# Four gate/up pairs in the direct form instead of six, new order lists, and three of four block differences moved to VectorE

## The reference

```
x = x + 0.5 * swiglu(rms(x, g_ffn1), w_up1, w_down1)      # FFN 1
...  projections, window attention, Fourier branch, gates, w_out ...
x = x + 0.5 * swiglu(rms(x, g_ffn2), w_up2, w_down2)      # FFN 2
out = rms(x, g_final)

swiglu(h, w_up, w_down): gate, up = split(h @ w_up, 2); (silu(gate) * up) @ w_down
```

## Time and profile before

| | |
|---|---|
| time, median of 3 runs | 988.93 us (988.77 to 989.03) |
| the profiled execution | 989.37 us, of which 987.6 us are the span of the trace |
| PE busy | 979.5 us, 99% of the span |
| VectorE, ScalarE, GpSimd busy | 681.4, 444.6, 183.1 us |
| granted TensorE clock, mean | 0.998 of full speed |

### The profile page before, as it was taken

The page is one execution under the profiler, slowest core; times in us unless marked ns, Lnnn a source line. Parts: engine busy times, 40 slices in busy tenths (PEclk is TensorE's granted clock), DMA queues, the critical chain, the costliest instruction groups (busy, mean ns, idle before and its releaser), DMA issues.

```text
span 987.6 us, 16144 instructions
## 1 busy us (share of the span) xinstructions
PE 979.5 (99%) x5788; PEld 872.9 (88%) x5788; DVE 681.4 (69%) x937; ACT 444.6 (45%) x677; POOL 183.1 (19%) x106
## 2 busy tenths in 40 slices
PE   9999999999999999999999999999999999999997
PEld 8889999999888888888888888888999999988887
DVE  5897989999544346678884564479798989943322
ACT  6534444447323235458773343443354444642322
POOL 1332434330011010000000002242333434000101
PEclk9999999999999999999999999999999999999999
DMA  7513424223433364122123343331333332343222
GB/s 220 166 43 91 123 85 127 86 85 91 133 89 94 110 167 121 55 86 64 44 76 96 106 127 100 93 106 50 101 107 103 109 90 80 106 118 100 83 62 86
DMA packets 188743, 98.26 MB, mean 100 GB/s; under 512 B 13384, under 2 KB 186520, under 8 KB 188704
## 3 DMA queue, kind: packets, MB, share of 16 engines
q1 hardware_dynamic: 186736, 94.40, 32.7%
q10 hardware_dynamic: 1968, 3.35, 0.9%
HBM read 95.61 MB, written 2.11 MB: 99 GB/s over the span
## 4 chain that ended last, share of the span: by engine, by line
PE 98%; issue 1%; DMA 0%; DVE 0%; POOLq 0%; POOL 0%; DVEq 0%
PE bank L1580 19%; PE bank L1581 19%; PE bank L1590 19%; PE bank L1684 11%; PE bank L1680 11%; PE bank L1678 11%; PE bank L1899 1%; PE bank L1800 1%; PE bank L1801 1%; PE bank L1805 1%; PE bank L1585 1%; PE bank L1887 0%; PE bank L1886 0%; PE bank L1917 0%; PE bank L1914 0%
## 5 line engine op out<-in xcount | busy, mean ns | idle before, releaser
L614 ACT ACTIVATE w_hi<-raw 128x1024 fp32r<-128x1024 f32 (+2 forms) x202 | 181.5, 902 | 232.9 <-PE bank L1590 151.6
L1040 DVE TENSOR_TENSOR w_lo<-raw,w_hi 128x1024 fp32r<-128x1024 f32 (+2 forms) x138 | 147.8, 1074 | 137.7 <-ACT w_hi L614 136.0
L1680 PE MATMUL bank<-t_lo,w_hi 128*128 128x256 f32 x896 | 224.7, 283 | 0.0
L1678 PE MATMUL bank<-t_hi,w_hi 128*128 128x256 f32 x896 | 224.6, 283 | 0.0
L1680 PEld LDWEIGHTS bank<-t_lo,w_hi 128*128 128x128 f32 x896 | 172.0, 192 | 0.2
L1678 PEld LDWEIGHTS bank<-t_hi,w_hi 128*128 128x128 f32 x896 | 172.0, 192 | 0.2
L1684 PE MATMUL bank<-t_hi,w_lo 128*128 128x256 f32 x896 | 144.0, 283 | 0.0
L1580 PE MATMUL bank<-a_hi,w_hi 128*128 128x512 f32 (+1 forms) x374 | 140.1, 379 | 0.0
L1581 PE MATMUL bank<-a_lo,w_hi 128*128 128x512 f32 (+1 forms) x374 | 139.4, 377 | 0.0
L1684 PEld LDWEIGHTS bank<-t_hi,w_lo 128*128 128x128 f32 x896 | 123.6, 192 | 0.0
L1529 POOL TENSOR_TENSOR ssum<-ssum,sq 128x512 f32<-128x512 f32 x20 | 30.6, 1528 | 498.9 <-ACT sq L651 498.9
(11 more groups left out here) (244 smaller groups left out, 1481.1 us busy)
## 6 DMA issues: line engine op xcount, KB each, us to landing
raw<-in_w_down_dram SPq DMA_DIRECT2D x48, 384.0 KB, 3.0
raw_b<-in_w_up_dram SPq DMA_DIRECT2D x64, 256.0 KB, 3.6
raw<-in_w_up_dram SPq DMA_DIRECT2D x64, 256.0 KB, 3.6
raw<-in_w_up_dram SPq DMA_DIRECT2D x24, 512.0 KB, 3.8
raw<-in_w_in_dram SPq DMA_DIRECT2D x22, 512.0 KB, 3.7
raw<-in_w_down_dram SPq DMA_DIRECT2D x32, 128.0 KB, 2.2
raw<-in_w_out_dram SPq DMA_DIRECT2D x8, 512.0 KB, 3.4
x_rows<-in_x_dram SPq DMA_DIRECT2D x4, 512.0 KB, 6.6
```

The source lines that it names most:

```text
L614: return nc.scalar.activation(dst, src, ACT.Copy, scale=scale)
L1040: vec.tensor_tensor(w_lo[:, s, 0:nk, :], raw[:, s, 0:nk, :], w_hi[:, s, 0:nk, :].bitcast(F32), ALU.subtract).then_inc(w_lo_ready, 1)
L1678: nc.tensor.matmul(out_ap, w_hi[:, slot, at_ + k, :], hi[:, k, :], start=first and k == 0, stop=False, skip_group_check=not first)
L1680: nc.tensor.matmul(out_ap, w_hi[:, slot, at_ + k, :], lo_[:, k, :], start=False, stop=False, skip_group_check=not first)
```

## The change

`DIRECT` becomes 4, so each FFN has 8 direct granules and 18 window pairs. Three of the four block differences move from GpSimd to VectorE's list (`t_difference`), each between other work. The fourth (`T_3`) stays on GpSimd, with a semaphore of its own (`t3_formed`), and waits for all eight `normed_h`. Both lists of `direct_pairs` are reordered.

```diff
-DIRECT = 6
+DIRECT = 4
@@ ScalarE, direct_pairs, behind silu(r, 1) and direct_hi(r, 7)
-                direct_hi(r, 8)
...
-                direct_hi(r, 11)
...
-                silu(r, 5)
+                t_rounded(r, T_B11)
+                t_rounded(r, T_1)
+                t_rounded(r, T_B21)
+                t_rounded(r, T_2)
+                silu(r, 2)
+                group_hi(r, 0, G0)
+                t_rounded(r, T_4)
+                group_hi(r, 0, G1)
+                t_rounded(r, T_3)
+                silu(r, 3)
+                group_hi(r, 0, G2)
+                t_rounded(r, T_B22)
@@ VectorE, direct_pairs, behind gate(r, 1)
-                swish(r, 0)
-                direct_lo(r, 6)
...
-                swish(r, 5)
+                for i in range(HK):
+                    normed_h(nrm, i)
+                swish(r, 0)
+                up(r, 1)
+                sums(r, 0)
+                direct_lo(r, 6)
+                direct_lo(r, 7)
+                t_difference(r, 0)
+                for i in range(HK, DK):
+                    normed_h(nrm, i)
+                t_difference(r, 1)
+                swish(r, 1)
+                gate(r, 2)
+                t_difference(r, 2)
+                t_rest(r, T_B11)
+                t_rest(r, T_2)
+                up(r, 2)
+                swish(r, 2)
+                t_rest(r, T_B21)
+                group_lo(r, 0, G0)
+                gate(r, 3)
+                t_rest(r, T_4)
+                group_lo(r, 0, G1)
+                t_rest(r, T_1)
+                sums(r, 1)
+                up(r, 3)
+                group_lo(r, 0, G2)
+                t_rest(r, T_3)
+                swish(r, 3)
+                t_rest(r, T_B22)
@@ VectorE, new
+            def t_difference(r, i):
+                to, one, two = ((T_1, T_B12, T_B11), (T_2, T_B22, T_1), (T_4, T_B21, T_2), (T_3, T_B22, T_B12))[i]
+                dve.wait_ge(normed, 2 * HK * r + (HK if to == T_1 else 2 * HK))
+                if i in (1, 2):
+                    dve.wait_ge(t_formed, 3 * r + i)
+                vec.tensor_tensor(t_sum[:, to, :, :], t_sum[:, one, :, :], t_sum[:, two, :, :],
+                                  ALU.subtract).then_inc(t_formed, 1)
@@ GpSimd
-                    for i, (to, one, two) in enumerate(((T_1, T_B12, T_B11), (T_2, T_B22, T_1), (T_4, T_B21, T_2),
-                                                        (T_3, T_B22, T_B12))):
-                        ...
+                    pool.wait_ge(normed, 2 * HK * (r + 1))
+                    nc.gpsimd.tensor_tensor(t_sum[:, T_3, :, :], t_sum[:, T_B22, :, :], t_sum[:, T_B12, :, :],
+                                            ALU.subtract).then_inc(t3_formed, 1)
```

More of the change, by code:

```diff
@@ L409, in build @@
         cos_copied, y_hi_ready, m_hi_ready = sem("cos_copied"), sem("y_hi_ready"), sem("m_hi_ready")
-        rows_squared = sem("rows_squared")
+        rows_squared, t3_formed = sem("rows_squared"), sem("t3_formed")
         last_squared, y_rows_ready, scaled_act = sem("last_squared"), sem("y_rows_ready"), sem("scaled_act")
@@ L729, in direct_pairs @@
                     act.dma_start(bias_rows, bias_row[:, :]).then_inc(bias_stored, 16)
-                t_rounded(r, T_B11)
-                direct_hi(r, 8)
                 t_rounded(r, T_1)
                 t_rounded(r, T_B21)
-                direct_hi(r, 9)
                 t_rounded(r, T_2)
                 silu(r, 2)
+                group_hi(r, 0, G0)
                 t_rounded(r, T_4)
-                direct_hi(r, 10)
+                group_hi(r, 0, G1)
                 t_rounded(r, T_3)
+                silu(r, 3)
+                group_hi(r, 0, G2)
                 t_rounded(r, T_B22)
-                silu(r, 3)
-                direct_hi(r, 11)
[L743 to L746, removed]
-                silu(r, 5)
             def t_rounded(r, t):
                 act.wait_ge(normed, 2 * HK * r + (HK if t in (T_B11, T_1) else 2 * HK))
-                if t in (T_1, T_2, T_4, T_3):
-                    act.wait_ge(t_formed, 4 * r + 1 + [T_1, T_2, T_4, T_3].index(t))
+                if t in (T_1, T_2, T_4):
+                    act.wait_ge(t_formed, 3 * r + 1 + [T_1, T_2, T_4].index(t))
+                if t in (T_3, T_B22):
+                    act.wait_ge(t3_formed, r + 1)
                 copy(t_hi[:, t, :, :], t_sum[:, t, :, :]).then_inc(t_hi_ready, 1)
@@ L1139, in direct_pairs @@
                 gate(r, 1)
-                swish(r, 0)
-                direct_lo(r, 6)
-                up(r, 1)
                 for i in range(HK):
                     normed_h(nrm, i)
-                swish(r, 1)
+                swish(r, 0)
+                up(r, 1)
+                sums(r, 0)
+                direct_lo(r, 6)
                 direct_lo(r, 7)
+                t_difference(r, 0)
                 for i in range(HK, DK):
                     normed_h(nrm, i)
-                direct_lo(r, 8)
+                t_difference(r, 1)
+                swish(r, 1)
                 gate(r, 2)
+                t_difference(r, 2)
+                t_rest(r, T_B11)
+                t_rest(r, T_2)
                 up(r, 2)
                 swish(r, 2)
-                t_rest(r, T_B11)
-                t_rest(r, T_2)
-                direct_lo(r, 9)
+                t_rest(r, T_B21)
+                group_lo(r, 0, G0)
                 gate(r, 3)
-                t_rest(r, T_B21)
+                t_rest(r, T_4)
+                group_lo(r, 0, G1)
+                t_rest(r, T_1)
+                sums(r, 1)
                 up(r, 3)
-                direct_lo(r, 10)
+                group_lo(r, 0, G2)
+                t_rest(r, T_3)
                 swish(r, 3)
[L1161 to L1169, removed]
-                t_rest(r, T_B22)
[L1171 to L1175, removed]
-                swish(r, 5)
+                t_rest(r, T_B22)
             def normed_h(n, m):
@@ L1183, in normed_h @@
                                          op0=ALU.mult, op1=ALU.mult).then_inc(normed, 1)
+            def t_difference(r, i):
[5 more added lines that the diff above has]
+                                  ALU.subtract).then_inc(t_formed, 1)
             def t_rest(r, t):
-                users = {T_B11: 1, T_1: 2, T_2: 3, T_B21: 3, T_4: 3, T_3: 4, T_B22: 4}
-                dve.wait_ge(t_formed, 4 * r + users[t])
+                users = {T_B11: 1, T_1: 2, T_2: 3, T_B21: 3, T_4: 3, T_3: 3, T_B22: 3}
+                dve.wait_ge(t_formed, 3 * r + users[t])
                 dve.wait_ge(t_hi_ready, len(T_HI_ORDER) * r + T_HI_ORDER.index(t) + 1)
```

## The result

The changed kernel takes 999.41 us (998.01 to 999.67, four runs), the kernel before 988.85 us beside it (988.63 to 989.03). The ratio is 1.0104, with a 95% interval of 1.0087 to 1.0122: slower, by 10.6 us. The forecast was 994.4 us with a range of 990.9 to 998.6. The direction is right, and the time lies 5.0 us above the forecast and 0.8 us above the range.

The account below looks back on a forecast made before the run. The prediction took PE, busy 99% of the span, as the bound. Per FFN, matmuls -1.60 and waits +4.3 gave +2.7 us, both +5.4; 988.93 + 5.5 = 994.4 us, range 990.9 to 998.6.

Parts of the forecast that it names:

- The matmuls: Two pairs per FFN go from direct (10.88 us) to window form (10.08 us): 1.60 us less per FFN, 3.20 both.
- What PE needs earlier: PE reaches window pair 0 at 56.61 us, not 78.37, so G2*T_3 needs u2 by 63.80 us.
- VectorE's list and the holds: VectorE's list before u2, 31.9 us undisturbed, loses 5.4 us to GpSimd's port holds; u2 ends near 68.1 us.
- The mark of `T_3`: On VectorE at 44.4 us, a swish lengthened to 2.8 us from 0.7 while GpSimd forms T_3.
- The five losses: VectorE's delays from five GpSimd instructions before u2: 2.2, 0.5, 1.1, 0.5 and 1.1 us, in all 5.4.
- The loads of pair 0: In FFN 1 they land at about 35.0 us, 1.0 us before sums(0) reaches them at 36.0.
- The waits of PE: Per FFN 4.3 us: 0.4 near 59.5 us on ScalarE's p_t copy, 3.9 before G2*T_3 near 63.8 us.
- The clock: Rival: PE's 3.9 us wait lowers the clock, costing about 2 us per FFN; 996.5 to 998.5 us, chance 0.18.
- a granted clock below 1.00 at 60 to 80 us: Sign around PE's long wait in FFN 1 that, if seen, makes the forecast wrong.
- The lists were not met: Rival: GpSimd's holds before u2 cost nothing that counts, u2 ends 1.1 us early; 985.7 us, chance 0.09.
- no half of the disturbance: Rival: 3 of 5.4 us of holds before u2 remain, a 1.9 us wait per FFN; 989.5 us, chance 0.08.

Follow-up runs that it names:

- experiment 7: Changed kernel, pair 0's loads earlier in FFN 1, its weight sums on VectorE before the first gate, T_3 on VectorE, T_B22 and swish(3) behind u2: 985.80 us.
- experiment 3: Changed kernel, swish(3) and t_rest(T_B22) moved on VectorE from ahead of u2 of pair 0 to behind pair 1's first group_lo: 994.36 us.
- experiment 2: Changed kernel, 10 matmuls into an unused bank ahead of the wait for u2 of pair 0 in each FFN: 996.97 us.
- experiment 4: Changed kernel, the fourth block difference (T_3) on VectorE too, so GpSimd makes none: 997.75 us.
- experiment 5: Changed kernel, all four block differences back on GpSimd, the new lists otherwise kept: 1002.44 us.

## Why the prediction was right in direction and short in size

**The matmuls, -3.2 us.** Right. The pace of window pairs stays 10.08 us behind pair 1, and experiment 7, in which PE loses only 0.6 us, is 3.2 us faster than the kernel before.

**What PE needs earlier.** Right: pair 0 at 56.48 (56.61), G2*T_3 due 7.19 us later, at 63.67.

**VectorE's list and the holds.** Right in every part, as VectorE's timeline of the changed kernel shows:

```profile
30.20 0.69 DVE L1107 TENSOR_TENSOR ga_t<-bank,rstd 128x512 f32<-128x512 f32 x1
...
43.23 1.22 DVE L1180 TENSOR_TENSOR t_sum<-t_sum 128x1024 f32<-128x1024 f32 x1
44.38 2.89 DVE L1120 TENSOR_TENSOR a_t<-gb_t,ub_t 128x512 f32<-128x512 f32 x1
47.20 0.68 DVE L1107 TENSOR_TENSOR ga_t<-bank,rstd 128x512 f32<-128x512 f32 x1
47.80 1.72 DVE L1180 TENSOR_TENSOR t_sum<-t_sum 128x1024 f32<-128x1024 f32 x1
49.44 3.45 DVE L1040 TENSOR_TENSOR t_lo<-t_sum,t_hi 128x1024 fp32r<-128x1024 f32 x2
...
62.21 1.72 DVE L1206 TENSOR_TENSOR w_lo<-raw_b,w_hi 128x1024 fp32r<-128x1024 f32 x1
63.85 2.30 DVE L1040 TENSOR_TENSOR t_lo<-t_sum,t_hi 128x1024 fp32r<-128x1024 f32 x1
66.07 0.68 DVE L1120 TENSOR_TENSOR a_t<-gb_t,ub_t 128x512 f32<-128x512 f32 x1
66.67 1.21 DVE L1040 TENSOR_TENSOR t_lo<-t_sum,t_hi 128x1024 fp32r<-128x1024 f32 x1
67.81 0.41 DVE L1213 TENSOR_TENSOR u_t<-bank,p_t 128x256 f32<-128x256 f32 x1
```

and GpSimd's beside it:

```profile
43.28 3.45 POOL L1536 TENSOR_TENSOR t_sum<-t_sum 128x1024 f32<-128x1024 f32 x1 [19.79 <-DVE t_sum L1171]
46.68 1.76 POOL L1543 TENSOR_TENSOR raw_b<-raw_b 128x512 f32<-128x512 f32 x1
48.52 2.15 POOL L1545 TENSOR_TENSOR raw_b<-raw_b 128x512 f32<-128x512 f32 x1
61.17 1.68 POOL L1543 TENSOR_TENSOR raw<-raw 128x512 f32<-128x512 f32 x1 [10.50 <-DVE raw L1196]
62.92 2.15 POOL L1545 TENSOR_TENSOR raw<-raw 128x512 f32<-128x512 f32 x1
```

A `t_difference` on VectorE takes 1.22 us, as `t_rest` does. The mark of `T_3`, a `swish` of 2.89 us at 44.38, was forecast as 2.8 at 44.4. The five losses are 2.2, 0.5, 1.1, 0.5 and 1.1 us: 5.4. `u2` ends at 68.22, forecast 68.1. The loads of pair 0 were in time: `sums(0)` ran without a wait at 35.86. The Trainium skill, SBUF — State Buffer, section "SBUF: two separate sides", has the loser of the shared port pair block for the other's whole instruction. These rows agree in kind, and VectorE's `swish` ends at 47.27 and needs 0.68, so it was free again 0.14 us before GpSimd's recorded end at 46.73, as the prediction took it.

**The waits of PE.** Right in kind and place, 0.4 us per FFN too small. The two waits are on the instructions named, 0.6 and 3.7 us (0.4 and 3.9 forecast; the recorded sum for the first, 56.9 + 0.6 + 1.9 + 0.4, gives 59.8 and not 59.9). The forecast took the end of `u2` less the due time, 68.1 - 63.80 = 4.3. It was 68.22 - 63.67 = 4.55. PE started 0.06 us after `u2` ended and its second matmul was 0.10 late: 4.7.

**The clock. This step failed.** The sum puts the clock at nothing. It measured 3.9 us, the larger part of the 4.6 by which the profiled execution (999.37) exceeds the 994.8 forecast for it. The prediction has the clock only as a rival, "if a spell is as long as the wait, it costs about 2 us per FFN", with a total of 996.5 to 998.5 and a chance of 0.18. This is what happened, in both FFNs, and a granted clock below 1.00 at 60 to 80 us is one of the signs by which the prediction itself calls the forecast wrong. Two things in it:

- Its chance was wrong. The earlier trace rows show the clock falling about 2.1 us after the last matmul ended (at 981.96; a mean of 0.53 over 984 to 986 leaves the upper level until about 984.1). A forecast standstill of 3.9 us outlasts that by far. So the row spoke for the fall, and "PE is dense up to the wait" was a weak reason against it: PE was busy all of 974 to 980, too, and 1.27 us of 980 to 982. It should have been part of the sum.
- Its size came out right by luck. It takes a spell as long as the wait, with half of it lost. The spells lasted 3.4 us, of which PE lost 1.5, and 6.8 us, of which PE lost 2.45, since it stood in the first 1.2: 3.9 us for the rival's 4. The time lies above the rival's 998.5 and above the range because the waits were 0.8 us longer in all as well, and the two never stood in one sum.

Against the profiled execution of before the terms as measured close: 989.37 - 3.2 + 9.4 + 3.9 - 0.1 = 999.4, for 999.37.

**The rivals that did not happen.** The lists were not met, and no half of the disturbance fell away: each hold that the prediction counted is there.

What stays open is which executions get a spell of 3.4 us and which one of 6.8. The changed kernel's second run took 998.01 us with a mean granted clock of 0.995, where the profiled one has 0.993; that fits a shorter time at the lower level, which no profile shows.

## What to carry to other kernels

Where one engine is busy 99% of the span, price a new wait twice: its length, and what the clock does behind it. Here a standstill of 3.6 us cost 3.8 us and then 1.4 to 2.7 more, and the same work cut into waits of at most 2 us cost nothing extra in the profiled run; if a wait can't be removed, splitting it, or filling it with idle matmuls, was worth 4.5 to 5 us over both FFNs. And when a change makes the bounding engine faster at a stage's start, look first for work on the other engines that can be done before the stage (here four weight sums in an idle stretch) rather than for a better order within it: reordering alone (experiment 3) gave back 0.8 of the 9.4 us of waiting, taking work out of the list as well (experiment 7) gave back 8.9.

## What the runs showed of the hardware that was not expected

- The fall of the clock follows the standstill with a delay that differs. In FFN 1 PE stopped at 64.7 and the clock fell at 69.1, 0.8 us after PE had started again at 68.28; in FFN 2 PE stopped at 684.5 and it fell at 686.9, while PE stood. Starting again before the fall did not avert it.
- A standstill of 2.4 us was enough for it (experiment 2), in one of the four runs not, by its time and its mean clock of 0.998; the waits of 1.8 us in experiment 3 did not bring it in the profiled run, and its other three runs took no longer than that one (994.02 to 994.42, for 994.55), though one of them has a mean clock of 0.994.
- Behind a wait, a spell at the lower level lasted 3.4 us or 6.8 us, in all eight cases of four profiles (the changed kernel, experiments 2, 4 and 5).
- Half the clock did not mean half the pace: matmuls of 256 columns followed each other after 0.213 us at the lower level and after 0.120 us at the upper one, so PE lost 44% of the time that it worked there.
